# Weight slots 64 bytes behind the moving tiles' place modulo 512 in place of 64 ahead, and rows of 258 columns 1,536 bytes apart, in a two-layer diffusion backbone

## What is computed

```python
# layer 0, all 512 tokens
xr, yr, qkv, z, beta, alpha = split(h @ w_in)        # 1024 -> 1024, 1024, 3072, 1024, 32
... gated linear recurrence and a delta-rule recurrence in chunks of 64 ...
xs = xs + g1 * (concat(lru, dn) @ w_out)             # 2048 -> 1024
xs = xs + g2 * (square(relu(h @ w1)) @ w2)           # 1024 -> 4096 -> 1024
# layer 1
q, k, v = split(h @ w_qkv)                           # q for the 256 latent tokens alone
xs = xs + g1 * (attend(q, k, v) @ w_o)
xs = xs + g2 * (square(relu(h @ w1)) @ w2)           # latent tokens alone
return rms_norm(xs, final_g)
```

## The kernel before

| tile | start before | modulo 512 | role |
|---|---|---|---|
| `w_hi`, `w_lo` | 60032, 68224 | 128 | weights |
| `w_hi2`, `w_lo2` | 81472, 89664 | 64 | weights |
| `h_hi`, `h_lo`, `hid_*`, `mix_*`, `head_lo`, `att_*` | 97856 and more | 64 | moving, 256 columns (1,024 bytes) a matmul |
| `up_hi`, `up_lo` row 0 | 196160, 212544 | 64 | moving, 258 columns (1,032 bytes) a matmul |
| `up_hi`, `up_lo` row k | 1,088 bytes apart | 64 + 64k | the same |

## Time and profile before

### The profile page before, as it was taken

One profiled execution on the slowest core, in us unless ns is written; L12 is line 12 of the kernel. 1 busy time (PEld: TensorE's weight loads), 2 busy tenths in 40 slices (PEclk: granted clock), 3 DMA queues, 4 the chain that ended last, 5 costly groups with the idle time before them and its releaser, 6 DMA issues.

```text
span 1370.0 us, 28118 instructions
## 1 busy us (share of the span) xinstructions
PE 1348.0 (98%) x11256; PEld 1274.6 (93%) x11256; DVE 854.5 (62%) x1308; ACT 701.8 (51%) x1135; POOL 288.6 (21%) x296
## 2 busy tenths in 40 slices
PE   6999999999999999999999999999999999999998
PEld 4899999998899999999999999999999988999998
DVE  4655789985455655542587666566736666765563
ACT  4368888878544455422543322333226665663553
POOL 2000224223566786621100000000020000200002
PEclk9999999999999999999999999999999999999999
DMA  9733232322410111123456566555423321656562
GB/s 327 202 82 89 78 93 78 93 78 70 140 38 32 62 33 32 63 78 101 139 187 198 184 189 197 185 185 184 139 93 123 98 73 32 192 175 203 173 194 78
DMA packets 138030, 170.88 MB, mean 125 GB/s; under 512 B 10912, under 2 KB 121760, under 8 KB 137920
## 3 DMA queue, kind: packets, MB, share of 16 engines
q1 hardware_dynamic: 137312, 169.13, 39.5%
q0 software_dynamic: 608, 0.19, 0.1%
HBM read 168.25 MB, written 1.05 MB: 124 GB/s over the span
## 4 chain that ended last, share of the span: by engine, by line
PE 93%; ACT 2%; DVE 2%; DMA 1%; POOL 1%; SPq 1%; issue 1%; DVEq 0%; ACTq 0%; POOLq 0%
PE bank L2535 63%; PE bank L2542 7%; PE bank L2949 3%; PE bank L2937 3%; PE bank L2966 1%; PE bank L2461 1%; DMA raw<-in_even_w_in 1%; PE bank L3188 1%; PE bank L2891 1%; PE bank L3211 1%; PE bank L2772 1%; PE bank L2915 1%; PE bank L2813 1%; PE bank L2798 1%; PE bank L2926 1%; PE bank L2878 1%
## 5 line engine op out<-in xcount | busy, mean ns | idle before, releaser
L1657 DVE TENSOR_TENSOR w_lo<-raw,w_hi 128x1024 fp32r<-128x1024 f32 x212 | 265.1, 1252 | 310.5 <-ACT w_hi L915 310.1
L915 ACT ACTIVATE w_hi<-raw 128x1024 fp32r<-128x1024 f32 x212 | 223.6, 1055 | 380.3 <-PE bank L2535 374.8
L2535 PE MATMUL bank<-h_hi,w_hi 128*128 128x256 f32 x1472 | 300.8, 282 | 5.7 <-DVE w_lo L1657 3.2
L2535 PE MATMUL bank<-h_hi,w_lo 128*128 128x256 f32 x1472 | 294.6, 278 | 0.0
L2535 PE MATMUL bank<-h_lo,w_hi 128*128 128x256 f32 x1472 | 289.2, 279 | 0.0
L2535 PEld LDWEIGHTS bank<-h_hi,w_hi 128*128 128x128 f32 x1472 | 226.7, 189 | 14.7 <-issue 10.6
L2535 PEld LDWEIGHTS bank<-h_hi,w_lo 128*128 128x128 f32 x1472 | 225.8, 188 | 0.0
L2535 PEld LDWEIGHTS bank<-h_lo,w_hi 128*128 128x128 f32 x1472 | 223.5, 189 | 0.3 <-DVE h_lo L1918 0.2
L2535 PE MATMUL bank<-hid_hi,w_hi 128*128 128x256 f32 x768 | 173.5, 280 | 0.0
L2535 PE MATMUL bank<-hid_hi,w_lo 128*128 128x256 f32 x768 | 172.2, 278 | 0.0
L2535 PE MATMUL bank<-hid_lo,w_hi 128*128 128x256 f32 x768 | 172.1, 278 | 0.0
(11 more groups left out here) (363 smaller groups left out, 2491.2 us busy)
## 6 DMA issues: line engine op xcount, KB each, us to landing
raw<-in_mlp_w SPq DMA_DIRECT2D x128, 512.0 KB, 3.6
late_w<-in_w_mod SPq DMA_DIRECT2D x56, 512.0 KB, 4.4
raw<-in_even_w_in SPq DMA_DIRECT2D x48, 512.0 KB, 3.8
raw<-in_w_mod SPq DMA_DIRECT2D x24, 512.0 KB, 4.4
first_w<-in_w_mod SPq DMA_DIRECT2D x16, 512.0 KB, 11.6
raw<-in_even_w_out SPq DMA_DIRECT2D x16, 512.0 KB, 3.4
raw<-in_attn_w_qkv SPq DMA_DIRECT2D x16, 512.0 KB, 3.6
raw<-in_attn_w_o SPq DMA_DIRECT2D x8, 512.0 KB, 3.5
```

The source lines that it names most:

```text
L915: act.activation(stored(w_hi, j, four), raw[:, j % RAW], ACT.Copy).then_inc(hi_ready, 1)
L1657: dve.tensor_tensor(stored(w_lo, j, four), raw[:, j % RAW], stored(w_hi, j, four).bitcast(F32), ALU.subtract).then_inc(split_done, 1)
L2535: return pe.matmul(bank[2 * pair + t][:, c - n0:c - n0 + CTX], w_[:, k, t * P:(t + 1) * P], x_[:, c:c + CTX], start=(kk == 0 and first and ...
```

## The change

The small tiles (`modv` to `gate_bias`) are placed ahead of the large ones, the place is then rounded up to a multiple of 512, and `xT`, `raw`, `w_hi`, `w_lo` and the space of the second pair follow. All weight slots now start at 0 modulo 512. `free`, from which the moving tiles are placed, comes 64 bytes later and has the same address as before (97856, 64 modulo 512). So every weight tile stands 64 bytes behind its moving tile's place modulo 512. The row of `up_hi` and `up_lo` grows from 272 to 384 elements, 1,536 bytes, so that each row starts at 64 modulo 512 too. `d_last`, 16 numbers a partition, gets no place of its own; it lies in a free part of `sp_x`. No instruction is added, taken out or moved on any engine; they differ in addresses alone.

```diff
-SHIFT, UP_ROW = 2, 272
+ALIGNED, BEHIND = 512, 64
+SHIFT, UP_ROW = 2, 384
...
         vec = place("vec", [NVEC])
-        xT = place("xT", [KT, T])
-        raw = place("raw", [RAW, UNIT_K, UNIT_C])
-        w_hi = place("w_hi", [SPLIT, UNIT_K, UNIT_C], F32R)
-        w_lo = place("w_lo", [SPLIT, UNIT_K, UNIT_C], F32R)
         modv = place("modv", [2, 6, 8, 2])
...
-        d_last = place("d_last", [2, 2, 4])
+        d_last = sp_x[:, 32:48].rearrange("p (t d c) -> p t d c", t=2, d=2)
         beta_gap = sp_x[:, 0:32].rearrange("p (n h) -> p n h", h=8)
         beta_p = sp_p[:, 0:64].rearrange("p (s d h) -> p s d h", d=2, h=8)
+        base[0] = (base[0] + ALIGNED - 1) // ALIGNED * ALIGNED
+        xT = place("xT", [KT, T])
+        raw = place("raw", [RAW, UNIT_K, UNIT_C])
+        w_hi = place("w_hi", [SPLIT, UNIT_K, UNIT_C], F32R)
+        w_lo = place("w_lo", [SPLIT, UNIT_K, UNIT_C], F32R)
         mod_off = base[0]
         base[0] += 16384
         w_hi2 = at("w_hi2", mod_off, [SPLIT, UNIT_K, UNIT_C], F32R)
         w_lo2 = at("w_lo2", mod_off + 8192, [SPLIT, UNIT_K, UNIT_C], F32R)
-        free = base[0]
+        free = base[0] + BEHIND
```

## The result

The changed kernel takes 1382.95 us (median of 6 runs, 1380.61 to 1385.23) against 1371.63 us for the kernel before in the same measurements (6 runs, 1370.59 to 1373.42). The ratio is 1.0077, with a 95% interval of 1.0067 to 1.0088. The profiled execution is the fastest of the six, 1380.61 us with a span of 1378.8; the one before had 1370.0, so the two traces differ by 8.8 us.

The account below looks back on a forecast made before the run. The prediction took TensorE's matmul count times pitch as the bound. Terms of 5.8, 3.2 and 5.4 us, less a 1 us remnant, gave 13.4 off 1371.8, 1358.4; with 0.8 for the median, 1359 us, range 1352 to 1383.

Parts of the forecast that it names:

- What bounds the kernel: Whole kernel: time is the number of matmuls times their pitch; TensorE is 93% of the last chain of waits.
- The distance decides: All large products: places of weights and moving tile modulo some power of two set the pitch, 113.3, 117.9 or 120.0 ns.
- (a): Rows of 258 columns: 768 matmuls at 120.8 ns lose their 7.5 ns over the floor, 5.8 us.
- the floor: Large products: the fast pitch of 113.3 ns, taken as the shortest; the sum over it is 19.9 us.
- (b): Second pair of slots, layer 1's down products and q: 480 matmuls lose 6.7 ns each, 3.2 us.
- the third rival: Large products: 64 behind shows the same two pitches as 64 ahead, as often; 1369.4 us, chance 0.14.
- (c): First pair of slots where it runs at 117.9 ns: 10.9 us over the floor, half of it, 5.4, won.
- the likeliest case: Large products: (a) and (b) lose their loss, (c) half, 1 us remains; 13.4 us won, chance 0.32.
- the lower bound: Steady runs at 64 behind: cost of 0 over the floor, against an upper bound of 6.7 ns per matmul.
- The slower rival: Some 4,850 matmuls at the floor go to a slower pitch: 1392 us at 117.9 ns, 1409 at 120.0; chance 0.24.
- The window named as the first to look at: Window 600 to 660: fewer than 528 matmuls would mean the floor is lost and the forecast's sign wrong.
- The side term: Recurrence, 256 plain fp32 matmuls whose tiles move by 64 bytes: up to 1.7 us lost or won, taken as 0.

Follow-up runs that it names:

- e2_ahead: From the changed kernel, moving tiles 448 bytes behind the rounded place, so all weights stand 64 bytes ahead: 1368.56 us, ratio 0.9984.
- e3_same: From the changed kernel, every moving tile at the same place modulo 512 as the weights (0 behind): 1405.07 us, ratio 1.0252.
- e4_shift: From the changed kernel, weights and moving tiles both 64 bytes higher, distance still 64 behind: 1383.44 us, ratio 1.0101.
- the four of the second group: From the changed kernel, weights 128, 192, 256 or 384 bytes behind: 1399.49, 1368.03, 1405.20 and 1398.68 us.

## Why the prediction was wrong, point by point

- **What bounds the kernel**: right for the MLPs, not for all. The three pitches, 113.3, 117.8 and 120.0 ns, came back in the runs at distances of 0 and 64, and in no window was the pitch under 113.1 ns. But in layer 0's input products a faster pitch is mostly eaten by waits. Over 1,584 large matmuls there (55.84 to 257.59 before) the steps of under 140 ns stand, added up, 4.6 us over 113.3 ns before and 1.2 in e2_ahead, 3.4 less; the longer steps within the runs grow from 0.9 to 3.5 us over it, and the whole is only 0.8 us shorter (201.75 and 200.99; the three later traces at 64 ahead have 200.8 to 201.0). Where the profile names what such a pause waits for, it is the split of the weights:

```profile
252.84 0.50 PE L2537 MATMUL bank<-h_hi,w_hi 128*128 128x256 f32 x2 [0.32 <-DVE w_lo L1659]
```

- **The distance decides**: right, and shown by e2_ahead, e3_same, e4_shift and the four of the second group. The cost repeats every 256 bytes, which the prediction didn't use.
- **(a)**: the loss of 5.8 us in the rows of 258 columns was to go, with over 345 matmuls in a window of 40 us. There were 340. Their pitch went from 120.8 to between 118 and 119; 768 x 2 = 1.5 us. Mis-sized: the floor isn't reached there at any of the distances tried.
- **(b)**: 3.2 us were to go, with the pitch at 113.3; it went from 120.0 to 117.8, 480 x 2.2 = 1.1 us. With (a) it makes up the 2.2 us that layer 1's MLP won, and the third rival, "the same two pitches", had sizes near these, 2.2 and 1.0.
- **(c)**: of its 10.9 us, 5.4 were to be won. Nothing was: layer 1's first pair stayed at 117.8, the window 160 to 290 holds 1,008 matmuls as before, where over 1,030 were wanted, and 112 to 132, fast before, went from 179 to 172. By e2_ahead even a fast pitch would have won little there, for the waits above.
- **The step that failed**: the likeliest case put the loss on the some 4,850 matmuls already at 113.3 ns at nothing, though the prediction had said that no row shows a steady run at 64 behind. It held that a distance with two pitches would show them about as the trace before did. The two pitches are the same at 64 behind, but most breaks of layer 0's MLP lead into the other one: 2,640 of its 3,072 matmuls went from 113.3 to 117.8 (most of the rest were at 117.8 before), which at 4.4 ns are the 11.5 us. The row from which I leaned to the lower bound, 120 ns behind against 123 ahead for six matmuls, holds for the rows of 258 columns (steady runs have 118.9 behind and 121.1 ahead) and says nothing of those of 256, where the order is the other way round.
- **The slower rival**: right in sign and in its floor-to-117.8 mechanism, too big at 1392, since it moved all 4,850; the long run of the out product (532 matmuls in its window), most of z, and v kept the fast pitch. Its own measure, a mean pitch over 115.7 ns, was passed: over all 8,448, steps of over 140 ns left out, it was 115.7 ns before and 117.1 in the changed kernel. The window named as the first to look at, 600 to 660, holds 532 and gave no warning: the floor was lost elsewhere.
- **The side term**: nothing. `d_r` with `d_tf` is still at 277 ns and `d_vn` with `d_at` at 275, as the earlier trace rows.

**Left open.** That the weight load and the moving read meet in SBUF is how I read the distances; no row shows such a meeting. Nor is it shown why the `late_row` break leads to the fast pitch at 64 ahead and to the slow one at 64 behind, and why one program enters the first up half fast in one execution and slow in another. How short a pause can be and still set the pitch anew was not tried.

## What to carry to other kernels

Where back-to-back matmuls are the bound, look at the distance between starts, not at busy time, and look at it by segment: here equal instructions had 113.3, 117.8 or 120.0 ns by where the weight tile lies against the moving tile modulo 256 bytes. Try the distances in runs (0, 32, 64 and so on); a guess from the nearest one measured had the wrong sign, and the best, 64 ahead, was 14 us from its mirror image and 25 from its neighbour at 32 ahead. When one distance shows two pitches, the mean over it isn't a property of the distance: count at how many entries each is taken, and treat an edit of anything between large products, a short wait included, as one that may flip what follows. And where a faster TensorE overtakes the engine that makes its weight tiles, as in the input products here, a shorter pitch buys a longer wait.

## What the hardware did that I had not expected

- The cost of a distance repeats every 256 bytes: 128 and 384 behind differ by 0.8 us, 0 and 256 by 0.1 us, over a scale of 37 us between the best and the worst.
- It is not symmetric: 64 ahead takes 1368.6 us and 64 behind 1383, though both know the same two pitches.
- A pitch once entered stays for hundreds of matmuls (720 over 85 us in the changed kernel). It can change behind matmuls of another kind, or behind a pause between two starts (steps of 0.21 and 0.30 us did it), and a program may take one or the other at the same place from run to run.
